# Expert products with 112 stationary columns in place of 128

## The chip, the cores and the metric

The kernel runs on one core of one Trainium2 chip. The metric is the time in device microseconds (us) of one execution; the time before is the median of three runs. TensorE multiplies; VectorE, ScalarE and GpSimd do elementwise work; SyncE issues the transfers from device memory.

## What is computed

The model has a batch of one, 256 tokens of width 1024 and two layers of a first block (half feed-forward layers, attention in the even layer, an RWKV-7 mixer in the odd one), followed by a second block of two layers: a mixer of pooling and convolution, a layer norm, then a dense SwiGLU in layer 0 and a mixture of experts in layer 1, a layer norm and a gated per-layer input. The change is in the mixture of experts:

```python
def moe_swiglu(h, w_router, w1, w3, w2):
    t = h.reshape(B * S, D)                                  # 256 tokens, D = 1024
    logits = (t @ w_router).astype(jnp.float32)
    top_vals, top_idx = lax.top_k(logits, TOP_K)             # 2 of 8 experts for each token
    top_w = jax.nn.softmax(top_vals, axis=-1)
    gates = jnp.sum(jax.nn.one_hot(top_idx, N_EXPERTS) * top_w[..., None], axis=1)
    out = jnp.zeros_like(t)
    for e in range(N_EXPERTS):                               # hidden width D_FF_EXPERT = 3584
        out = out + gates[:, e:e + 1] * swiglu_2(t, w1[e], w3[e], w2[e])
    return out.reshape(B, S, D)
```

All is in fp32. The expert weights alone are 8 x 3 x 1024 x 3584 numbers, 352 MB of the 610 MB that the kernel moves.

## The kernel before, in words

**Rounded fp32 in three products.** Every large product is made of operands in a rounded fp32 type that TensorE streams in one pass. ScalarE writes the rounded high part of a weight block (`split_hi`, line 421), VectorE the rest (`split_lo`, line 429), and `mm3` (line 448) issues three matmuls through `mm` (line 439): high by high, high by low, low by high. Each matmul instruction has a weight load (LDWEIGHTS, PEld in the rows) of the stationary operand, then the moving operand is streamed. In the expert products the moving operand is the weights, 512 columns wide, and the stationary one is the tokens of one expert.

**The stream of weights.** The SyncE queue (line 3561) loads units of 1024 KB into five raw slots, each load waiting until the unit that held its slot has been split. Each unit is split in two halves of 128 x 1024, and four buffers of split halves stand between the splitting engines and TensorE (semaphores `w_hi_ready`, `w_ready`, and `w_read` back).

**Two ways through the experts.** `route_vector` finds the two experts of each token and the largest number of tokens that any expert has, and compares it with `tile_limit`. `either` loads the flag on each compute engine. If it is set, the general way runs (`all_tensor` and its partners): every expert is applied to all 256 tokens. If not, the own way runs (`own_tensor`, `own_scalar`, `own_vector`): the tokens of an expert are gathered into at most 128 slots by products with a 0/1 matrix (`own_gather_tensor`, two experts at a time), and the results are scattered back by products with its transpose, the missing slots being zeros in it.

**The order of the work in the own way.** An expert has 14 blocks of 256 hidden columns, so there are 112 iterations. For each block n, TensorE runs `products(n, 0)` (12 matmuls: 4 depth tiles of 128, three each, into one 512-column bank for both w1 and w3), `turn(n - 1)` (two plain fp32 transposes of the activated block, line 3266), `products(n, 1)` (12 matmuls), and `down(n - 1)` (12 matmuls: 2 halves of the block, 2 halves of the 1024 outputs, three each). Scatters come in four blocks after some experts, a gather in one block of every second expert. ScalarE applies silu (line 3386), rounds the turned block (3356), and copies the gated output y (3373); VectorE multiplies by the w3 half (3436), subtracts for the low part of the turned block (3407) and of y (3414), and adds scattered parts (3424). These read and write all 128 rows of their tiles. The last block has its own `last_down` and `last_scatter`.

The three places where an expert's tokens are the stationary operand are in `products`, `down` and `last_down`. Their column count is 128 whatever number of slots is taken.

Of the kernel before, what the change touches and what calls it, by code (L numbers as in the profile page):

```python
# [13 lines left out]
P = 128  # L14
D = 1024
T = 256
KT = D // P
# [4 lines left out]
CHUNK = 256  # L22
# [17 lines left out]
PAD_POOL = 16  # L40
ALPHA = 4.0 ** 0.25
ARENA = 23296
RAW_SLOTS = 3
MORE_SLOTS = 2
MORE_RAW_AT = 9 * KT * T
# [188 lines left out]
class Kernel:  # L234


    def __init__(self, nc, ctx, dram, out):
# [3 lines left out]
        def sb(name, cols, dtype=F32):  # L241
            return ctx.enter_context(nc.sbuf_tensor(name, [P, cols], dtype))
# [7 lines left out]

        self.raw = sb("raw_weights", RAW_SLOTS * UNIT)
        def sb_rounded(name, cols):
# [20 lines left out]
        self.arena_at = nc.sbuf_base  # L273
        self.arena = sb("arena", ARENA)
        self.x_hi, self.x_lo = self.rounded_arena("own_x_hi", 3, KT * T), self.rounded_arena("own_x_lo", 7, KT * T)
# [11 lines left out]
        mixes = [self.arena[:, at * UNIT:(at + 1) * UNIT] for _, _, at in AFTER_MIXES.values()]  # L287
        self.raw_slots = [self.raw[:, i * UNIT:(i + 1) * UNIT] for i in range(RAW_SLOTS)] + more + mixes
        self.slot_landed = [sem(f"slot_landed{i}") for i in range(RAW_SLOTS + MORE_SLOTS + len(AFTER_MIXES))]
        self.w_hi_ready, self.w_ready, self.w_read = sem("weights_hi_ready"), sem("weights_ready"), sem("weights_taken")  # L290
# [49 lines left out]
    def place_units(self):  # L340

        first = min(n for n, (name, _, _) in enumerate(self.stream) if name.startswith("exp_"))
        self.first_wide = first
        turn = [RAW_SLOTS + i for i in range(MORE_SLOTS)] + [(first - len(AFTER_MIXES) + i) % RAW_SLOTS for i in range(RAW_SLOTS)]
        self.slot, self.landing, self.before = [], [], []
        held = [[] for _ in self.raw_slots]
        placed = 0
        for n, (name, i, _) in enumerate(self.stream):
            if (name, i) in AFTER_MIXES:
                slot = RAW_SLOTS + MORE_SLOTS + list(AFTER_MIXES).index((name, i))  # L350
            else:
                slot = placed % RAW_SLOTS if n < first else turn[(n - first) % len(turn)]
                placed += 1
# [94 lines left out]
def mm3(k, dst, w, at, src, src_at, start, stop, shared, moving_weights=False):  # L448
    for i, (a, b) in enumerate(((0, 0), (0, 1), (1, 0))):
        lhsT, rhs = (src[b][:, src_at], w[a][:, at]) if moving_weights else (w[a][:, at], src[b][:, src_at])  # L450
        ins = mm(k, dst, lhsT, rhs, start and i == 0, stop and i == 2, shared)
    return ins
# [464 lines left out]
EXPERT_UNITS = D_FF_EXPERT // CHUNK  # L917
# [87 lines left out]
class AttentionTiles:  # L1005
    def __init__(self, k):
# [10 lines left out]
        at += 4 * T  # L1017
        self.work = k.arena[:, at:ARENA]
        cols = 2 * N_GROUPS * T + 4
# [442 lines left out]
class RwkvTiles:  # L1462
    def __init__(self, k):
# [14 lines left out]
        self.root, self.inverse = k.arena[:, at:at + 8], k.arena[:, at + 8:at + 16]  # L1478
        self.masks = k.arena[:, ARENA - N_RW_MASK * RW_CHUNK:ARENA]
        self.tmp, self.kk, self.kk2 = (k.xn[:, 2 * i * T:2 * (i + 1) * T] for i in range(3))  # L1480
# [895 lines left out]
def tap_matrix(k, i):  # L2376
    at = ARENA - 4 * TE_TAPS * P
    return k.arena[:, at + i * P:at + (i + 1) * P]
# [450 lines left out]
E = N_EXPERTS  # L2829
# [408 lines left out]
def own_tensor(k):  # L3238
    t = MoeTiles(k)
    mt, sc, ve = k.own_mm, k.own_act, k.own_dve  # L3240
    ident = k.con("ident")
    banks = OwnBanks(k, START_BANKS)
    spare_bank = banks.next

    def products(n, part):

        e, i = divmod(n, EXPERT_UNITS)
        bank = k.bank[4 + n % 2]
        for s in range(2):
            j = k.half[EXPERT_IN, 2 * n + part, s]  # L3250
            k.pe.wait_ge(k.w_ready, j + 1)
            if i == 0 and e % 2 == 0:
                k.pe.wait_ge(*sc.at(("gathered", e // 2, 2 * part + s)))
                k.pe.wait_ge(*ve.at(("gathered", e // 2, 2 * part + s)))
            for k2 in range(2):
                kt = 4 * part + 2 * s + k2
                at = kt * T + e % 2 * P
                ins = mm3(k, bank[:, :], k.weights(j), slice(k2 * 2 * CHUNK, (k2 + 1) * 2 * CHUNK),
                          t.tokens[e // 2 % 2], slice(at, at + P), kt == 0, kt == KT - 1, False, True)
            ins.then_inc(k.w_read, 1)  # L3260

    def turn(n):
        k.pe.wait_ge(*ve.at(("product", n)))
        bank = spare_bank(ve.at(("hidden", n)))
        for i in range(2):
            ins = k.pe.transpose(bank[:, i * P:(i + 1) * P], k.act_buf[:, n % 2 * T + i * P:n % 2 * T + (i + 1) * P], ident)  # L3266
        ins.then_inc(*mt.step(("turned", n)))

    def down(n):
        e, i = divmod(n, EXPERT_UNITS)  # L3270
        y0 = 2 * (e % 2)
        for s in range(2):
            j = k.half[EXPERT_DOWN, n, s]
            k.pe.wait_ge(k.w_ready, j + 1)
            k.pe.wait_ge(*ve.at(("hidden", n)))
            if i == 0 and s == 0 and e >= 2:
                k.pe.wait_ge(*ve.at(("y", e - 2, 1)))
            for c in range(2):
                at = n % 2 * T + s * P
                ins = mm3(k, k.bank[y0 + c][:, :], k.weights(j), slice(c * 512, (c + 1) * 512), k.hidden,  # L3280
                          slice(at, at + P), i == 0 and s == 0, i == EXPERT_UNITS - 1 and s == 1, True, True)
            ins.then_inc(k.w_read, 1)

    def last_down():
        halves = [k.half[EXPERT_DOWN, last, s] for s in range(2)]
        k.pe.wait_ge(k.w_ready, halves[1] + 1)
        k.pe.wait_ge(*ve.at(("hidden", last)))
        for c in range(2):
            for s in range(2):
                at = last % 2 * T + s * P  # L3290
                ins = mm3(k, k.bank[2 * ((E - 1) % 2) + c][:, :], k.weights(halves[s]), slice(c * 512, (c + 1) * 512),
                          k.hidden, slice(at, at + P), False, s == 1, True, True)
            ins.then_inc(*mt.step(f"y{c}"))

    def last_scatter():
        e, before = E - 1, SCATTER_AFTER[E - 1] - 1
        for c in range(2):
            for tt in range(TT):
                u = 2 * c + tt
                k.pe.wait_ge(*ve.at(("z", before, u)))  # L3300
                if c:
                    k.pe.wait_ge(*ve.at(("y", e, tt)))
                moe_z_tensor(k, u, False)
            k.pe.wait_ge(*ve.at(("y", e, c)))
            k.pe.wait_ge(*sc.at(("back", e)))
            for tt in range(TT):
                for low in range(2):
                    ins = mm(k, k.bank[SUM_BANKS[2 * c + tt]][:, :], t.back[e % 4][:, tt * P:(tt + 1) * P],
                             quarter(t.y_own[e % 2][low], c), False, low == 1, True)
                ins.then_inc(k.moe_summed, 1)  # L3310

    def scatter(g, u):
        bank, group = spare_bank(ve.at(("z", g, u))), SCATTERED[g]
        for e in group:
            c, tt = divmod(u, 2)
            if tt == 0:
                k.pe.wait_ge(*ve.at(("y", e, c)))
                k.pe.wait_ge(*sc.at(("back", e)))
            for low in range(2):
                ins = mm(k, bank[:, :], t.back[e % 4][:, tt * P:(tt + 1) * P], quarter(t.y_own[e % 2][low], c),  # L3320
                         e == group[0] and low == 0, e == group[-1] and low == 1, True)
        ins.then_inc(*mt.step(("z", g, u)))

    last = E * EXPERT_UNITS - 1
    for n in range(last + 1):
        e, i = divmod(n, EXPERT_UNITS)
        if n >= 2:
            k.pe.wait_ge(*ve.at(("product", n - 2)))
        products(n, 0)
        if n > 0:  # L3330
            turn(n - 1)
        products(n, 1)
        if n > 0:
            down(n - 1)
        if e - 1 in SCATTER_AFTER and 3 <= i < 7:
            scatter(SCATTER_AFTER[e - 1], i - 3)
        if i == GATHER_AT and e % 2 and e < E - 1:
            own_gather_tensor(k, t, e // 2 + 1, banks)
    turn(last)
    per_layer_input_tensor(k, 1, 0, 1)  # L3340
    last_down()
    last_scatter()
    per_layer_input_tensor(k, 1, 1, 3)
# [217 lines left out]
        k.sp.dma_start(k.raw_slots[k.slot[n]][0:rows, 0:cols], src).then_inc(k.slot_landed[k.slot[n]], 16)  # L3561


def bass_macaron_attention_rwkv_conv_moe_kernel(nc, dram, out, tile_limit=P):
    with ExitStack() as ctx:
        k = Kernel(nc, ctx, dram, out)
        for real in (False, True):
            k.begin(real)
            tensor_program(k)
            scalar_program(k)  # L3570
            vector_program(k, tile_limit)
            gpsimd_program(k)
            sync_program(k)
# [93 lines left out]
```

## Time and profile before

| what | value |
|---|---|
| median of 3 runs | 2622.1 us (2621.82 to 2622.3) |
| span of the profiled execution, first to last instruction | 2622.8 us |
| TensorE busy, share of the span | 2590.1 us, 99% |
| VectorE, ScalarE, GpSimd busy | 2029.8, 1604.4, 237.8 us |
| moved by DMA | 609.58 MB, mean 232 GB/s |

The profiled execution's own time is its span, 0.7 us above the median. The last two fifths of the span, from about 1600 us, are the experts; there the slices of the page show 349 to 375 GB/s, the last one excepted, and TensorE at nine tenths or more in each slice. In rows of the trace, PE is a matmul and PEld the load of its stationary operand; `128*128` is rows by stationary columns, and the shape behind it that of the moving operand. The end of a matmul is modelled and overlaps the next one's start, so the distance between starts tells the pace, not the duration.

### The profile page before, as it was taken

To read this page: it belongs to the slowest core of one execution; us is meant where nothing else is said; L and a number is where in the kernel's file an instruction comes from. 1 tells how busy PE (TensorE), PEld (TensorE's weight loads), DVE (VectorE), ACT (ScalarE), POOL (GpSimd) and SP (SyncE) were. 2 spreads that over 40 slices of the span, in tenths; PEclk is the share of its full clock that TensorE was granted. 3 is DMA by queue.
4 is the path that set the end of the run, shared out by engine and by line. 5 is a ranking of instruction groups with operands and counts; after the bars stand their busy time and mean duration, and the time that the engine had idled before them with its cause. 6 is when DMAs were issued, how large, how long until landed. Compare 5 with 4: busy or idle time off the path is not lost.

```text
span 2622.8 us, 42218 instructions
## 1 busy us (share of the span) xinstructions
PE 2590.1 (99%) x17004; PEld 2230.8 (85%) x17004; DVE 2029.8 (77%) x2919; ACT 1604.4 (61%) x2362; POOL 237.8 (9%) x236
## 2 busy tenths in 40 slices
PE   8999999999999999999999999999999999999999
PEld 7999899999977779999888888888888888888887
DVE  6667676776755547668756787999999999999997
ACT  5557655555542235553555536887788778787875
POOL 1101000000111208002510010000000000000000
PEclk9999999999999999999999999999999999999999
DMA  7554355455321134562455535999999999999994
GB/s 268 188 183 146 111 193 179 175 193 193 126 97 51 66 126 170 180 226 104 173 185 189 188 136 200 375 368 351 361 365 369 349 349 371 372 364 353 373 365 164
DMA packets 85383, 609.58 MB, mean 232 GB/s; under 512 B 9608, under 2 KB 9864, under 8 KB 12224
## 3 DMA queue, kind: packets, MB, share of 16 engines
q1 hardware_dynamic: 82080, 594.58, 61.9%
q10 hardware_dynamic: 2752, 9.09, 1.0%
q8 instruction: 138, 2.26, 0.3%
q0 software_dynamic: 352, 3.15, 0.3%
q14 instruction: 61, 0.50, 0.1%
HBM read 605.73 MB, written 1.05 MB: 231 GB/s over the span
## 4 chain that ended last, share of the span: by engine, by line
PE 94%; DVE 4%; ACT 1%; issue 1%; DMA 0%; ACTq 0%; DVEq 0%
PE bank L439 93%; PE bank L3266 1%; DVE weights_lo L429 0%; ACT weights_hi L421 0%; DMA x_T<-in_x 0%; DVE mean L580 0%; PE bank L2139 0%; DVE rstd L496 0%; DVE weights_hi_scratch L2323 0%; ACT squares L478 0%; DVE weights_hi_scratch L2283 0%; DVE arena L589 0%; DVE x_T L905 0%; DVE arena L2625 0%; DVE source L663 0%
## 5 line engine op out<-in xcount | busy, mean ns | idle before, releaser
L429 DVE TENSOR_TENSOR weights_lo<-raw_weights,weights_hi 128x1024 fp32r<-128x1024 f32 x816 | 1003.0, 1249 | 358.0 <-ACT weights_hi L421 352.5
L421 ACT CAST weights_hi<-raw_weights 128x1024 fp32r<-128x1024 f32 x816 | 847.5, 1050 | 302.7 <-PE bank L439 284.2
L439 PE MATMUL bank<-source,weights_hi 128*128 128x512 f32 (+1 forms) x2464 | 613.7, 365 | 13.7 <-ACT weights_hi L421 10.1
L439 PEld LDWEIGHTS bank<-source,weights_hi 128*128 128x128 f32 x2464 | 412.8, 190 | 60.4 <-ACT weights_hi L421 10.1
L439 PE MATMUL bank<-weights_hi,source 128*128 128x512 f32 (+1 forms) x1280 | 387.3, 386 | 1.5 <-DVE source L663 1.0
L439 PE MATMUL bank<-source,weights_lo 128*128 128x256 f32 x2112 | 380.4, 282 | 0.0
L439 PEld LDWEIGHTS bank<-source,weights_lo 128*128 128x128 f32 x2112 | 338.3, 190 | 37.7 <-DVE weights_lo L429 0.3
L429 DVE TENSOR_TENSOR weights_lo<-arena,weights_hi 128x1024 fp32r<-128x1024 f32 x278 | 335.9, 1224 | 30.7 <-ACT weights_hi L421 27.1
L421 ACT CAST weights_hi<-arena 128x1024 fp32r<-128x1024 f32 x278 | 292.2, 1053 | 50.7 <-PE bank L439 36.1
L439 PEld LDWEIGHTS bank<-weights_hi,source 128*128 128x128 f32 x1280 | 231.5, 188 | 45.4 <-issue 3.1
L439 PE MATMUL bank<-weights_lo,source 128*128 128x512 f32 (+1 forms) x640 | 243.4, 380 | 0.0
L439 PE MATMUL bank<-weights_hi,hidden_hi 128*128 128x512 f32 x536 | 209.2, 390 | 0.0
L439 PE MATMUL bank<-weights_lo,hidden_hi 128*128 128x512 f32 x536 | 208.7, 389 | 0.0
L439 PE MATMUL bank<-hidden_hi,weights_hi 128*128 128x256 f32 x736 | 208.7, 284 | 0.0
L439 PE MATMUL bank<-weights_hi,hidden_lo 128*128 128x512 f32 x536 | 208.7, 389 | 0.0
L439 PE MATMUL bank<-hidden_lo,weights_hi 128*128 128x256 f32 x736 | 208.3, 283 | 0.0
L439 PE MATMUL bank<-hidden_hi,weights_lo 128*128 128x256 f32 x736 | 208.2, 283 | 0.0
L439 PE MATMUL bank<-weights_hi,other_source_hi 128*128 128x512 f32 x448 | 180.4, 403 | 0.0
L439 PE MATMUL bank<-weights_lo,other_source_hi 128*128 128x512 f32 x448 | 175.5, 392 | 0.0
L439 PE MATMUL bank<-weights_hi,other_source_lo 128*128 128x512 f32 x448 | 174.6, 390 | 0.0
L439 PE MATMUL bank<-arena,raw_weights 128*128 128x256 f32 (+2 forms) x592 | 145.6, 397 | 0.0
L439 PEld LDWEIGHTS bank<-hidden_hi,weights_hi 128*128 128x128 f32 x736 | 141.2, 192 | 0.5 <-issue 0.3
(350 smaller groups left out, 3382.4 us busy)
## 6 DMA issues: line engine op xcount, KB each, us to landing
raw_weights<-in_exp_in SPq DMA_DIRECT2D x134, 1024.0 KB, 6.5
arena<-in_exp_in SPq DMA_DIRECT2D x90, 1024.0 KB, 6.7
raw_weights<-in_exp_w SPq DMA_DIRECT2D x67, 1024.0 KB, 6.6
arena<-in_exp_w SPq DMA_DIRECT2D x45, 1024.0 KB, 6.6
raw_weights<-in_ffn_w_down SPq DMA_DIRECT2D x44, 1024.0 KB, 4.9
raw_weights<-in_ffn_w_up SPq DMA_DIRECT2D x43, 1024.0 KB, 4.8
raw_weights<-in_ffn_w_gate SPq DMA_DIRECT2D x42, 1024.0 KB, 4.8
raw_weights<-in_dense_w SPq DMA_DIRECT2D x33, 1024.0 KB, 4.8
```

The lines of the kernel that those rows point to most:

```text
L421: k.act.copy(k.weights(j)[0], raw_half(k, j)).then_inc(k.w_hi_ready, 1)
L429: k.dve.tensor_tensor(lo, raw_half(k, j), hi.bitcast(F32), ALU.subtract).then_inc(k.w_ready, 1)
L439: return k.pe.matmul(dst, lhsT, rhs, start=start, stop=stop, skip_group_check=shared)
L3266: ins = k.pe.transpose(bank[:, i * P:(i + 1) * P], k.act_buf[:, n % 2 * T + i * P:n % 2 * T + (i + 1) * P], ident)
```

## The change

The stationary operand of the expert products takes the first 112 slots in place of 128, and the results are written to the first 112 partitions of their banks. The limit above which the general way is taken is 112 tokens in place of 128. Gathers, transposes, scatters and the work of the other engines keep their shapes; partitions 112 to 127 of the banks keep what was in them, and their slots have zeros in the scattering matrix.

```diff
--- before.py
+++ after.py
@@ -40,6 +40,7 @@
 PAD_POOL = 16
 ALPHA = 4.0 ** 0.25
 ARENA = 23296
+OWN_SLOTS = 112
 RAW_SLOTS = 3
 MORE_SLOTS = 2
 MORE_RAW_AT = 9 * KT * T
@@ -3255,8 +3256,8 @@
             for k2 in range(2):
                 kt = 4 * part + 2 * s + k2
                 at = kt * T + e % 2 * P
-                ins = mm3(k, bank[:, :], k.weights(j), slice(k2 * 2 * CHUNK, (k2 + 1) * 2 * CHUNK),
-                          t.tokens[e // 2 % 2], slice(at, at + P), kt == 0, kt == KT - 1, False, True)
+                ins = mm3(k, bank[0:OWN_SLOTS, :], k.weights(j), slice(k2 * 2 * CHUNK, (k2 + 1) * 2 * CHUNK),
+                          t.tokens[e // 2 % 2], slice(at, at + OWN_SLOTS), kt == 0, kt == KT - 1, False, True)
             ins.then_inc(k.w_read, 1)
 
     def turn(n):
@@ -3277,8 +3278,8 @@
                 k.pe.wait_ge(*ve.at(("y", e - 2, 1)))
             for c in range(2):
                 at = n % 2 * T + s * P
-                ins = mm3(k, k.bank[y0 + c][:, :], k.weights(j), slice(c * 512, (c + 1) * 512), k.hidden,
-                          slice(at, at + P), i == 0 and s == 0, i == EXPERT_UNITS - 1 and s == 1, True, True)
+                ins = mm3(k, k.bank[y0 + c][0:OWN_SLOTS, :], k.weights(j), slice(c * 512, (c + 1) * 512), k.hidden,
+                          slice(at, at + OWN_SLOTS), i == 0 and s == 0, i == EXPERT_UNITS - 1 and s == 1, True, True)
             ins.then_inc(k.w_read, 1)
 
     def last_down():
@@ -3288,8 +3289,8 @@
         for c in range(2):
             for s in range(2):
                 at = last % 2 * T + s * P
-                ins = mm3(k, k.bank[2 * ((E - 1) % 2) + c][:, :], k.weights(halves[s]), slice(c * 512, (c + 1) * 512),
-                          k.hidden, slice(at, at + P), False, s == 1, True, True)
+                ins = mm3(k, k.bank[2 * ((E - 1) % 2) + c][0:OWN_SLOTS, :], k.weights(halves[s]),
+                          slice(c * 512, (c + 1) * 512), k.hidden, slice(at, at + OWN_SLOTS), False, s == 1, True, True)
             ins.then_inc(*mt.step(f"y{c}"))
 
     def last_scatter():
@@ -3561,7 +3562,7 @@
         k.sp.dma_start(k.raw_slots[k.slot[n]][0:rows, 0:cols], src).then_inc(k.slot_landed[k.slot[n]], 16)
 
 
-def bass_macaron_attention_rwkv_conv_moe_kernel(nc, dram, out, tile_limit=P):
+def bass_macaron_attention_rwkv_conv_moe_kernel(nc, dram, out, tile_limit=OWN_SLOTS):
     with ExitStack() as ctx:
         k = Kernel(nc, ctx, dram, out)
         for real in (False, True):
```


## Rows read from the trace of the kernel before

**Rows 1.** The page: span, busy time of each engine, and the chain that ended last.

```profile
span 2622.8 us, 42218 instructions
...
PE 2590.1 (99%) x17004; PEld 2230.8 (85%) x17004; DVE 2029.8 (77%) x2919; ACT 1604.4 (61%) x2362; POOL 237.8 (9%) x236
...
PE 94%; DVE 4%; ACT 1%; issue 1%; DMA 0%; ACTq 0%; DVEq 0%
```

**Rows 2.** Busy us by stretch in plain units; then PEclk, DMA share, GB/s.

```profile
1912.40:2038.90 126.50, 126.50 (x571) 103.92 (x571) 119.27 (x127) 103.99 (x122) 0.00 (x0) 1.00 0.98 367
```

**Rows 3.** The waits, 1700 to 2400 us; last line the DMA queue's: total, times, longest.

```profile
ACT weights_hi L421 <- PE bank L439: 53.2, 142, 1.3
DVE weights_lo L429 <- ACT weights_hi L421: 42.8, 124, 2.0
...
SPq L3561 <- DVE weights_lo L429: 617.6, 240, 7.5
```

**Rows 4.** The chain of waits in order of time: start us, us, what.

```profile
1633.54 0.22 PE bank L3266 x2
1633.75 8.21 PE bank L439 x36
1641.97 0.22 PE bank L3266 x2
```

**Rows 5.** Timeline of TensorE, first product and last: start us, us, what.

```profile
1607.64 0.71 PE L439 MATMUL bank<-weights_hi,source 128*128 128x512 f32 x2
...
2583.70 0.39 PE L439 MATMUL bank<-weights_lo,hidden_hi 128*128 128x512 f32 x1
```

**Rows 6.** Timeline of TensorE in one unit.

```profile
2004.79 0.38 PE L3266 MATMUL bank<-consts,activated 128*128 128x128 f32 x2
...
2005.24 0.40 PE L439 MATMUL bank<-weights_hi,other_source_lo 128*128 128x512 f32 x1
2005.47 0.40 PE L439 MATMUL bank<-weights_lo,other_source_hi 128*128 128x512 f32 x1
...
2007.78 0.39 PE L439 MATMUL bank<-weights_hi,hidden_hi 128*128 128x512 f32 x1
...
2010.50 0.39 PE L439 MATMUL bank<-weights_hi,other_source_hi 128*128 128x512 f32 x1
```

**Rows 7.** Timeline of TensorE, matmuls of 256 columns in the first layer.

```profile
105.17 0.28 PE L439 MATMUL bank<-hidden_lo,weights_hi 128*128 128x256 f32 x1
...
106.97 0.28 PE L439 MATMUL bank<-hidden_lo,weights_hi 128*128 128x256 f32 x1
```

**Rows 8.** Timeline of TensorE, plain fp32 matmuls.

```profile
965.69 5.34 PE L439 MATMUL bank<-arena,raw_weights 128*128 128x256 f32 x24
970.87 1.89 PE L439 MATMUL bank<-arena 128*128 128x256 f32 x8
```

**Rows 9.** Weight loads over the span by form: count, busy us, mean ns, idle.

```profile
L439 PEld LDWEIGHTS bank<-weights_hi,hidden_hi 128*128 128x128 f32 x536 | 100.6, 188 | 21.4 <-issue 0.5 <-DVE weights_lo L429 0.3
...
L439 PEld LDWEIGHTS bank<-arena,raw_weights 128*128 128x128 f32 x544 | 98.3, 192 | 15.7 <-issue 1.8
...
L439 PEld LDWEIGHTS bank<-weights_lo_scratch 64*64 64x64 f32 x496 | 21.4, 135 | 2.9 <-issue 1.6 <-DVE weights_lo_scratch L2280 0.7 <-DVE weights_lo_scratch L2266 0.5
```

**Rows 10.** Timeline of weight loads in the same unit.

```profile
2007.78 0.19 PEld L439 LDWEIGHTS bank<-weights_hi,hidden_lo 128*128 128x128 f32 x1
```

**Rows 11.** Groups of VectorE by form, 1700 to 2400 us: busy, mean ns, idle.

```profile
L429 DVE TENSOR_TENSOR weights_lo<-arena,weights_hi 128x1024 fp32r<-128x1024 f32 x192 | 232.1, 1224 | 19.4 <-ACT weights_hi L421 17.0
...
L3407 DVE TENSOR_TENSOR hidden_lo<-bank,hidden_hi 128x256 fp32r<-128x256 f32 x80 | 33.4, 417 | 0.0
L3436 DVE TENSOR_TENSOR activated<-activated,bank 128x256 f32<-128x256 f32 x80 | 33.1, 414 | 0.0
...
L3414 DVE SCALAR_TENSOR_TENSOR own_y_lo<-bank,arena,own_y_hi 128x512 fp32r<-128x512 f32 x12 | 8.9, 746 | 0.0
```

## Prediction

> **What bounds the kernel now.** I read the page first: of a span of 2622.8 us TensorE is busy 2590.1, and the chain of work that ended last is 94% TensorE, nearly all of it the matmul helper [rows 1]. A busy share alone says little here, since matmul records overlap, so I went on to the stage that the change touches. The busy time by stretch shows, inside the expert loop, TensorE busy all of the time at a granted clock of 1.00 (its 2.4 GHz level), VectorE 94%, ScalarE 82%, and the DMA engines 98% at 367 GB/s: three resources stand close together, and the order has to be settled by waits [rows 2]. Between 1700 and 2400 us TensorE has no line in the list of waits at all. ScalarE waits 53.2 us for it (buffers of split weights that it has to give back), VectorE 42.8 us for ScalarE, and the DMA queue 617.6 us for VectorE to free a raw slot [rows 3]. So everything is paced by TensorE, and DMA has no wait of its own to give away: nobody waits for a landing. The chain repeats 36 matmuls in 8.21 us and two transposes in 0.22 us, from 1633.54 to 1641.97, a **unit of 8.43 us** [rows 4]. There are 8 x 14 = 112 such units, from 1607.64 to the last product at 2583.70 [rows 5]. The few units with a gather or scatter in them are longer by work that the change leaves alone.
>
> **What one matmul costs.** In the quiet half of a unit 12 matmuls start between 2007.78 and 2010.50: 0.2267 us each [rows 6]. 512 columns at 2.4 GHz are 0.2133 us, so 13.3 ns of each is something else. Matmuls of the same rounded type with 256 columns start every 0.120 us (15 from 105.17 to 106.97 [rows 7]); 256 columns are 0.1067, so the rest is again 13.3 ns: a price for each matmul, not for each moving column. Plain fp32 matmuls go through twice and start every 0.216 us (24 from 965.69 to 970.87 [rows 8]), which leaves only 2.5 ns. They load 128 columns too. After the two transposes the matmuls start further apart, 0.23 us or more (2005.24 to 2005.47), and from there to 2007.78 ten take 2.31 us, 0.231 each, before the pace settles at 0.2267 [rows 6]. By the arithmetic a unit is 0.218 for transposes, 36 x 0.2133 = 7.68 for streaming, and **0.535 us of remainder**.
>
> **The change, part by part.** Rounded and plain fp32 operands both stand as f32 in the rows; names tell them apart (arena with raw_weights is plain).
> Part 1, the loads. 4032 products (24 + 12 for each of 112 units) load 112 stationary columns for 128. A load of 128 columns takes 188 ns, one of 64 columns (plain fp32) 135 ns: 0.83 ns a column [rows 9]. I expect 188 - 13 = 175 ns. But a load starts together with a matmul (both at 2007.78) and has 0.227 us until the next [rows 6, 10]: even the 188 ns lie beside the stream with 39 to spare. Taken by itself this is worth nothing.
> Part 2, the 13.3 ns. No row has a rounded matmul with a load of other than 128 columns, so its dependence must be bounded. Below: it is a fixed handover of the array and nothing is saved, 0 us. Above that: it is what the load takes from the moving stream while both read, and goes with the loaded columns. Two things speak for this: the type that streams once leaves 13.3 ns and the one that streams twice, with slack, 2.5; and after a disturbance of the alignment (the transposes) the price is 18 ns for a while (0.231 less 0.2133), which a fixed handover would not show. Then 16/128 of 13.3 is 1.67 ns, x 4032 = **6.7 us**. The ends of this: with the 2.5 ns held fixed and the rest of the remainder scaled, (0.535 - 0.090)/8 x 112 = 6.2; with all of it scaled, 0.535/8 x 112 = 7.5. I take 6.7, the settled half of the unit being the cleanest row.
> Part 3, a quicker kind of load that could be lost. The loads of rounded and plain fp32 take 188 and 192 ns, and the step from 64 to 128 columns is the full 0.83 ns a column, so no faster kind of load is at work now that 112 columns could lose [rows 9]; my sum has no loss here. The Trainium skill ("TensorE: Matmul & The Clock Gate", Weight-path perf modes) says that a fast weight load is on only with exactly 128 stationary columns of a type that isn't FP32; if it were on here, this change would switch it off and loads could grow fourfold. These rows speak against it.
> Part 4, the rest. Matmuls write 112 partitions and stream the same 512 columns: 0. Transposes, gathers, scatters, ScalarE's and VectorE's reads stay at 128 rows: 0. No wait, semaphore or DMA is added or moved. The limit in the flag's comparison is another constant: 0, if the flag stays low (below).
> Part 5, who is late next. A unit shorter by 0.06 us (8.37) needs what the others can give: VectorE needs 6 x 1.224 + 0.417 + 0.414 = 8.175 us in a plain unit [rows 11], cover 0.26 now and 0.20 after; DMA at 98% allows about 2%, 0.17 us. Both still cover it. The two units in an expert with the 0.75 us of the lower half of y [rows 11] already run VectorE over a unit's length, and the four weight buffers carry it.
> Sum against the profiled 2622.8: -6.7, 2616.1. The median of the three runs shown is 2622.1, 0.7 less; on it **2615.4 us**. What a measurement can tell from no change is 0.2%, 5.2 us, so my term is just outside.
>
> **Rivals.**
> A, the forecast: the 13.3 ns go with the columns, 2614.6 to 2615.9.
> B, a fixed price: loads are 175 ns in the trace, but starts stay 0.2267 apart: 2622, give or take 1. For it: the settled value is the same to a tenth of a ns for 256 and 512 columns, as a handover would be. Against it: the unsettled 18 ns, the 2.5 of plain fp32.
> C, more than in proportion: 13.3 ns is also just what 16 columns take at 0.83 ns each, so if the stream waited for the last columns of a load, all of it could go, 4032 x 13.3 = 54 us. Against it stand the 39 ns of cover. It would not be given whole: DMA at 98% caps the stage of 976 us near 2%, 19 us, then ScalarE waits for landings: 2603.
> D, slower: the array must run empty when the column count changes, 128 to 112 and back around each pair of transposes. Place: before the transposes and before the first product after them. Price: a matmul's record lasts 0.39 us and the next starts after 0.227, so 0.16 us of it is overlap that an emptying lays bare [rows 6]; twice a unit, 224 x 0.16 = 36 us, 2658. It decides from 0.024 us an occurrence on. Against it: going from plain transposes back to rounded products costs now no such gap, from 2004.79 to 2005.24 there are 0.45 us for work of 0.43 [rows 6]. The Trainium skill ("TensorEngine Tiling (Array Packing)", Key Properties) says that a change of tiling mode drains TensorE; 112 columns are over 64 and so no other mode by its list, and no row here has 112.
> E, the change takes the other branch: with an expert above 112 tokens the general way runs. A unit is then 96 products of 0.120 and 24 of 0.227, 17.0 us for 8.43 [rows 6, 7], x 112 = 955 us more, 3577. The trace tells only that no expert has over 128. Worked out from the reference with its own first inputs the counts are 84, 108, 48, 52, 68, 36, 70, 46: 108 fits with four to spare. Other seeds of the same inputs give 128, 131 and 121, so this is a risk of the data.
>
> **How the numbers follow.** A 0.43, B 0.40, C 0.06, D 0.08, E 0.03. The likeliest is A, its own range 2614.6 to 2615.9. A and B together are 0.83, so the range needs both with their spread, 2614 to 2623.5; I take the low end down to 2611, since the ten unsettled matmuls of a unit may gain more than in proportion, and stop before C. Faster by over 0.2%: A but for a hundredth, and C, 0.48. Within: B and that hundredth, 0.41. Slower: D and E, 0.11.
>
> **What would show it.** In the profile after: 4032 loads at about 175 ns with 112 columns; in the quiet half of a unit starts 0.225 apart (A) or 0.2267 (B); a unit of 8.37 or 8.43; TensorE still without waits. C would show starts near 0.22 with ScalarE waiting for DMA. D would show 0.16 us gaps beside the transposes at line 3266, E the groups of the general way. I am wrong in the mechanism if loads don't shorten, or if the unit shortens while the quiet half's spacing does not.

## The result and the profile after

The changed kernel takes **2641.8 us** (median of 5 runs, 2639.4 to 2643.1) against 2622.1 (5 runs, 2621.8 to 2622.4): ratio **1.007**, 95% interval 1.006 to 1.0081. It is slower by 19.7 us where 6.7 less were forecast. The own way still runs. Profile against profile, one execution of each kernel, the spans differ by 17.6 us. The page of the kernel after, answering to [rows 1]:

```profile
span 2640.4 us, 42218 instructions
...
PE 2607.3 (99%) x17004; PEld 2177.6 (82%) x17004; DVE 2036.6 (77%) x2919; ACT 1603.1 (61%) x2362; POOL 238.1 (9%) x236
```

The same number of instructions; loads are busy 53 us less, and matmuls 17 us more. The weight loads by form, answering to [rows 9], and the busy time of the stretch of [rows 2]:

```profile
L440 PEld LDWEIGHTS bank<-weights_hi,hidden_hi 128*112 128x112 f32 x448 | 78.0, 174 | 25.8 <-issue 0.3 <-DVE weights_lo L430 0.3
```

```profile
1912.40:2038.90 126.50, 126.50 (x560) 94.90 (x559) 117.28 (x123) 100.78 (x119) 0.00 (x0) 1.00 0.97 361
```

A load takes 174 ns for 188, as it should. TensorE is again busy all of the time at its 2.4 GHz level, with 560 matmuls in the stretch for 571. Nobody else became late: VectorE, ScalarE and DMA all do less in the same time. The waits from 1700 to 2400 us, answering to [rows 3], have no line with TensorE waiting either:

```profile
ACT weights_hi L422 <- PE bank L440: 57.2, 142, 1.3
DVE weights_lo L430 <- ACT weights_hi L422: 46.8, 128, 2.0
```

So the matmuls themselves are slower. The chain, answering to [rows 4], and TensorE's timeline in the quiet half of a unit, answering to [rows 6]:

```profile
1694.09 0.22 PE bank L3267 x2
1694.30 8.39 PE bank L440 x36
1702.70 0.22 PE bank L3267 x2
```

```profile
2005.91 0.39 PE L440 MATMUL bank<-weights_hi,other_source_lo 128*112 128x512 f32 x1
2006.15 0.40 PE L440 MATMUL bank<-weights_lo,other_source_hi 128*112 128x512 f32 x1
2006.38 0.39 PE L440 MATMUL bank<-weights_hi,hidden_hi 128*112 128x512 f32 x1
2006.61 0.39 PE L440 MATMUL bank<-weights_hi,hidden_lo 128*112 128x512 f32 x1
...
2008.01 0.39 PE L440 MATMUL bank<-weights_hi,hidden_lo 128*112 128x512 f32 x1
```

The transposes still take 0.22 us, but the 36 products 8.39 us for 8.21: a unit is **8.61 us for 8.43**. From 2005.91 to 2008.01 nine matmuls start 0.2333 us apart, not 0.2267. The time above streaming has gone from 13.3 to 20.0 ns a matmul. In full resolution the starts follow a pattern of three distances, near 237, 231 and 232 ns, that runs through a whole unit and begins again after each pair of transposes. In the mean over the 36 products of a unit the distance has grown by 5.0 ns, not by 6.7, since 12 of the 36 stood at some 231 ns before. Of the 111 stretches from one pair of transposes to the next, 80 are 8.61 us, 14.3 us of the loss; all 111 together are 17.0 us longer.

One more thing stands in the same trace. After each of the three later gathers some units are quicker, with the very same instructions on the same tiles. The chain at such a place:

```profile
1811.38 8.26 PE bank L440 x36
1819.64 0.22 PE bank L3267 x2
1819.86 8.24 PE bank L440 x36
...
1836.80 8.40 PE bank L440 x36
```

Units of 8.46 and 8.48 us turn into one of 8.61 with nothing in the program different. The count of columns alone can't be the cause; the same matmuls run in one steady pattern or in another.

### The profile page after: what moved, and what is told of

The parts are those of the page before. It is cut to its first block, busy times and chain, and to the rows that moved or that the text cites. A ratio compares the mean times of both kernels' runs of the same rounds, so it can differ in the third digit from the quotient of the medians.

```text
span 2640.4 us, 42218 instructions
## 1 busy us (share of the span) xinstructions
PE 2607.3 (99%) x17004; PEld 2177.6 (82%) x17004; DVE 2036.6 (77%) x2919; ACT 1603.1 (61%) x2362; POOL 238.1 (9%) x236
## 4 chain that ended last, share of the span: by engine, by line
PE 94%; DVE 4%; ACT 1%; issue 1%; DMA 0%; POOL 0%; ACTq 0%; DVEq 0%
PE bank L440 92%; PE bank L3267 1%; DVE weights_lo L430 0%; ACT weights_hi L422 0%; DMA x_T<-in_x 0%; ACT squares L479 0%; DVE mean L581 0%; POOL squares L976 0%; PE bank L2140 0%; DVE rstd L497 0%; DVE weights_hi_scratch L2324 0%; DVE weights_hi_scratch L2284 0%; DVE arena L590 0%; DVE x_T L906 0%; DVE arena L2626 0%
## 5 line engine op out<-in xcount | busy, mean ns | idle before, releaser
L440 PE MATMUL bank<-weights_hi,source 128*112 128x512 f32 (+2 forms) x1280 | 389.2, 387 | 1.5 <-DVE source L664 1.0
L440 PEld LDWEIGHTS bank<-weights_hi,source 128*112 128x112 f32 (+1 forms) x1280 | 219.9, 179 | 59.2 <-issue 3.1
L440 PE MATMUL bank<-weights_lo,source 128*112 128x512 f32 (+2 forms) x640 | 245.4, 383 | 0.0
L440 PE MATMUL bank<-weights_lo,hidden_hi 128*112 128x512 f32 (+1 forms) x536 | 212.3, 396 | 0.0
L440 PE MATMUL bank<-weights_hi,hidden_hi 128*112 128x512 f32 (+1 forms) x536 | 211.3, 394 | 0.0
L440 PE MATMUL bank<-weights_hi,hidden_lo 128*112 128x512 f32 (+1 forms) x536 | 210.3, 392 | 0.0
L440 PE MATMUL bank<-weights_hi,other_source_hi 128*112 128x512 f32 x448 | 181.0, 404 | 0.0
L440 PE MATMUL bank<-weights_lo,other_source_hi 128*112 128x512 f32 x448 | 177.5, 396 | 0.0
L440 PE MATMUL bank<-weights_hi,other_source_lo 128*112 128x512 f32 x448 | 176.0, 393 | 0.0
```

Of the source, the lines that this page charges most:

```text
L440: return k.pe.matmul(dst, lhsT, rhs, start=start, stop=stop, skip_group_check=shared)
```

## The experiments

"Unit" below is the time from one pair of transposes to the next in a plain block, the median over an expert's plain units in the trace. The sweeps give each of the eight experts its own column count and first column; slots outside an expert's columns are left out of its products, and only the distances between starts are read. Each sweep has one profiled execution.

**How many columns.** The edit, here for s1 (s2 has 128, 100, 96, 88, 80, 72, 64, 48):

```diff
-OWN_SLOTS = 112
+COLS = (128, 124, 120, 116, 112, 108, 104, 96)
...
-                ins = mm3(k, bank[0:OWN_SLOTS, :], k.weights(j), slice(k2 * 2 * CHUNK, (k2 + 1) * 2 * CHUNK),
-                          t.tokens[e // 2 % 2], slice(at, at + OWN_SLOTS), kt == 0, kt == KT - 1, False, True)
+                ins = mm3(k, bank[0:COLS[e], :], k.weights(j), slice(k2 * 2 * CHUNK, (k2 + 1) * 2 * CHUNK),
+                          t.tokens[e // 2 % 2], slice(at, at + COLS[e]), kt == 0, kt == KT - 1, False, True)
```

> One kernel, eight column counts: experts 0 to 7 take 128, 124, 120, 116, 112, 108, 104 and 96 stationary columns in their products (limit for the general way back at 128; slots above an expert's count are left out of its products, and the trace is read, not the time). What is read is the mean distance between matmul starts in each expert's plain units. The trace of the changed kernel has 233.3 ns at 112 and 226.7 at 128. Theory 1, quadrants: a column count that isn't a multiple of 32 is dear, so 128 and 96 give 226.7 and all between 233. Theory 2, length: the price of a load on the moving stream changes steadily with its length, so the distance grows from 128 (226.7) over 120 (230) to 112 (233.3) and on to 104 (237) and 96 (240). Theory 3, lock: load and stream fall into a repeating pattern that depends on the count in no steady way; then the values jump, 112 is 233.3, and some counts repeat every three matmuls. Theory 4, drain at the change of shape: all distances inside a unit 226.7 and the loss beside the transposes; the trace after already speaks against it.

> As s1, with 128, 100, 96, 88, 80, 72, 64 and 48 columns for experts 0 to 7 (slots above that are left out). Theory 1, quadrants: 128, 96 and 64 at 226.7, the others near 233. Theory 2, length: 96 at 240, growing below. Theory 3, lock: jumps, no order. If what remains is the load's own reading taken from the stream, 64 and 48 must lie clearly below 226.7 (half the columns, at most 220).

Measured units, us: 128: **8.433**; 124: 8.444; 120: 8.608; 116: 8.607; 112: **8.613**; 108: 8.506; 104: 8.463; 100: 8.607; 96: 8.500; 88: 8.40 and 8.60; 80: 8.620; 72: 8.530; 64: 8.502; 48: 8.653. The 88 columns have no one value: their units alternate. The chain in s2:

```profile
1997.17 8.39 PE bank L443 x36
2005.56 0.22 PE bank L3270 x2
2005.78 8.18 PE bank L443 x36
```

The loads shorten evenly, 188 ns at 128 to 122 at 48. Theory 1 falls (96 and 64 are not 8.433), so does theory 2 (104 is better than 112, 100 worse than both), and with it the forecast: at 48 columns the distance is larger than at 128, so what a load reads isn't what the stream loses. Jumps without order are theory 3. The chain around a unit of 120 columns in s1:

```profile
1936.21 0.22 PE bank L3270 x2
1936.42 8.40 PE bank L443 x36
1944.82 0.22 PE bank L3270 x2
```

**Where the columns lie.** s3 and s6 add a first column other than 0:

```diff
-                at = kt * T + e % 2 * P
+                at = kt * T + e % 2 * P + FROM[e]
```

> Same number of columns, other place: experts 0 to 7 take (columns from offset) 128 from 0, 112 from 0, 112 from 16, 112 from 8, 112 from 4, 120 from 8, 96 from 0, 96 from 32, so that some loads end where the load of 128 ends; products then hold other slots than they should, with the same amount of work. Theory 5, place: the load is read from its last column or its price hangs on where it ends, so 112 from 16 and 120 from 8 give 226.7 and 112 from 0 gives 233.3, with 8 and 4 in between or elsewhere. Theories 1 to 3: the offset doesn't matter, all four of 112 give 233.3 and both of 96 the same.

> Finer steps and other starts, experts 0 to 7 (columns from offset): 126, 122, 118, 114, 110 from 0, then 120 from 4, 124 from 4, 116 from 12 (other slots than they should have in the last three). Lock theory: values between 226.7 and 236 in no order, neighbours of 2 columns differing by several ns, and for the same 120 columns a third value beside 233.3 (from 0) and 226.7 (from 8). A rule of the end (a load that ends on a multiple of 512 bytes is cheap) would give 226.7 for 124 from 4 and 116 from 12; 112 from 16 with 231.7 speaks against it already. A rule of the start would give 120 from 4 the 233.3 of 112 from 4.

Units, by the byte within the 512 of a slot block at which the load ends:

| ends at | columns from first column: unit, us |
|---|---|
| 512 | 128 from 0: 8.433; 124 from 4: 8.407; 120 from 8: 8.407; 116 from 12: 8.407; but 112 from 16: 8.555; 96 from 32: 8.555 |
| 496 | 124 from 0: 8.444; 120 from 4: 8.444 |
| 480 | 120 from 0: 8.608; 112 from 8: 8.608 |
| 464 | 116 from 0: 8.607; 112 from 4: 8.607 |

(126, 122, 118, 114 and 110 from 0: 8.620, 8.543, 8.566, 8.513, 8.603.) The same 120 columns give 8.608, 8.444 or 8.407. The chain for expert 5 of s3, 120 columns from 8, against that of s1 above, 8.19 for 8.40:

```profile
2313.55 0.22 PE bank L3270 x2
2313.77 8.19 PE bank L443 x36
2321.96 0.22 PE bank L3270 x2
```

Loads of different length that end at the same byte agree to a nanosecond a matmul or better in the mean, down to 116 columns at 512; the place of the start doesn't do that. The exception is kept: below 116 columns the end at 512 is no longer cheap, and 112 from 16 and 96 from 32 share another value. The forecast in s3 that 112 from 16 is cheap was a miss.

**Which products, which order.** In s4 only the products (`COLS`) or only the down products (`DOWN_COLS`) of an expert are narrowed; in s7 `mm3` takes its three products in another order:

```diff
-    for i, (a, b) in enumerate(((0, 0), (0, 1), (1, 0))):
+    for i, (a, b) in enumerate(order):
```

> Which products carry it: experts 0 to 7 take (gate and up products / down products) 128/128, 112/128, 128/112, 112/112, 112/112, 96/128, 128/96, 96/96 columns (slots above are left out). If the price belongs to each matmul with 112 columns, an expert with 112 only in the 24 gate and up products loses 24/36 of the full loss of 0.18 us a unit, 0.12, and one with 112 only in the 12 down products 0.06. If it is a lock that runs on over the whole unit, the two don't add up: the 128-column part is slower than 226.7 too while its partner is 112, or the 112-column part is not slow at all.

> Same loads and streams, other order of the three products of a group (in the kernel: high stationary x high moving, low x high, high x low). Experts 0 to 7: 128 columns in the orders hh hl lh, lh hh hl, lh hl hh (stationary named first); 112 columns in the same three; 120 and 108 columns in the first. If the price is the number of columns or of partitions written, order changes nothing: 226.7 at 128 and 233.3 at 112, in all orders. If it is a lock between the addresses or types that follow each other, values move: I expect one of the orders of 112 at another steady value (229 to 236) and 128 to lose its 226.7 in one of them.

s4: 112/128 8.526, 128/112 8.460, 112/112 8.613, against 8.433. The losses 0.093 and 0.027 don't add up to 0.180, nor are they 0.12 and 0.06: a matmul's price hangs on those around it. The other mixes say the same: 96/128 8.467, 128/96 8.493, 96/96 8.500. In 128/96 the down products alone run at about 230 ns. s7: nothing moves, 8.433 in all orders of 128, 8.613 in all of 112, 8.611 for 120 and 8.507 for 108. My expectation there was wrong; which rounded part follows which plays no role.

**The limit alone.**

```diff
-def bass_macaron_attention_rwkv_conv_moe_kernel(nc, dram, out, tile_limit=P):
+def bass_macaron_attention_rwkv_conv_moe_kernel(nc, dram, out, tile_limit=112):
```

> The other half of the change by itself: 128 columns, the flag's limit at 112. If the whole loss is the column count, this is the kernel before: 2622, ratio 1.000 within 0.001, a unit of 8.433 us. If the limit costs anything (another constant in one comparison), part of the 20 us shows here.

2622.7 us against 2622.7, ratio 1.000 (0.9991 to 1.001). The column count carries all.

**The address, without touching the columns.** A pad moves tiles in on-chip memory; s8 is a sweep with the pad, s9 has 128 columns throughout:

```diff
+        sb("pad_source", 8)
         source, scratch = sb_rounded("source", 2 * KT * T)
```

> A pad of 8 numbers (32 bytes a partition) ahead of the tokens' tile, so that this and every later tile lies 32 bytes further, while the split weights stay. Experts 0 to 7: 128, 124, 120, 116, 112 from 0, 112 from 16, 108, 96 columns. If the address of the stationary operand (against the weights or absolutely) decides, 120 now starts where 120 from 8 did and gives 226.7 and a unit of 8.407 in place of 233.3 and 8.608, and 128 may lose its 226.7. If only the place inside the 128 slots or the count decides, all values are those of s1: 226.7, 228, 233.3, 233.3, 233.3, 231.7, 230, 230.

> The kernel before, 128 columns everywhere, with only the 32-byte pad ahead of the tokens' tile. Theory of the address: the load of 128 columns then ends 32 bytes past a multiple of 512, as expert 0 of s8 (8.620 us a unit for 8.433), so this kernel loses 0.187 x 100 plain units and a like share of the others, about 20 us, 2642, as much as the change itself, with no column fewer. Other layers keep or move a little. Theory of the count: 2622, no difference.

s8: 128: 8.620; 124: 8.620; 120: 8.433; 116: 8.453; 112: 8.620; 112 from 16: 8.539; 108: 8.613; 96: 8.487. The quick place has moved with the pad, from 128 columns to 120, which now end at 512. It isn't quite the 8.407 that was expected from s3 for the same 120 columns: there only the reads of the products moved, here all later tiles did. s9 is the kernel before with the pad and nothing else; the chain in its experts:

```profile
1966.42 0.22 PE bank L3271 x2
1966.64 8.40 PE bank L444 x36
1975.04 0.22 PE bank L3271 x2
```

This kernel has not a column fewer than the one before and nearly the unit of the changed one, 8.62 us for 8.61. From the first transposes of the experts to the last it takes 982.0 us, where the kernel before takes 961.9 and the changed one 978.9: the loss of 20 us is there as forecast. Its time is 2634.9, ratio 1.0051 (1.0035 to 1.0066), not 2642, since the experts begin at 1604.1 us, where they begin between 1613.1 and 1617.2 in the profiles of all kernels with the tiles in their old places. So the other layers gained 9 us or more by the same pad, and their columns are the same, too; only addresses differ. Which operands make the other layers quicker was not looked into.

**One operand's address or the distance of the two.** s10 has the pad ahead of the split weights, so both operands move; s11 places the split weights behind the other tiles with 32 bytes before them, so that among the operands of the products only the moving one changes its place within 512 bytes. It also comes to lie some 139 KB further in the memory by the sizes in the kernel, the tiles ahead of it 32 KB less far, and the small tiles behind it (constants, the activated block) move by the 32 bytes, too; no run has that without the 32 bytes.

> The pad of 32 bytes ahead of the split weights, so that the moving and the stationary operands both lie 32 bytes further and keep their distance. Experts 0 to 7: 128, 124, 120, 116, 112, 108, 104, 96 columns. If the distance between the two operands decides, the values of s1 come back: 8.433 at 128, 8.608 at 120, 8.613 at 112. If the stationary operand's own address decides, those of s8: 8.620 at 128, 8.433 at 120, 8.620 at 112.

> Only the split weights (the moving operand) lie 32 bytes further against a multiple of 512; the stationary tiles keep theirs. Experts as in s10. If the stationary address alone decides, the values of s1 (8.433, 8.444, 8.608, 8.607, 8.613, 8.506, 8.463, 8.500). If the distance decides, others: 128 loses its 8.433.

| columns | 128 | 124 | 120 | 116 | 112 | 108 | 104 | 96 |
|---|---|---|---|---|---|---|---|---|
| s1, nothing moved | 8.433 | 8.444 | 8.608 | 8.607 | 8.613 | 8.506 | 8.463 | 8.500 |
| s10, both by 32 bytes | 8.433 | 8.444 | 8.611 | 8.607 | 8.613 | 8.506 | 8.463 | 8.500 |
| s8, stationary by 32 | 8.620 | 8.620 | 8.433 | 8.453 | 8.620 | 8.613 | - | 8.487 |
| s11, moving by 32 | 8.620 | 8.607 | 8.613 | 8.506 | 8.470 | 8.387 | 8.520 | 8.607 |

The same 116 columns in s1, s10, s8 and s11, one unit's products of the chain each:

```profile
1988.05 8.39 PE bank L443 x36
```

```profile
1988.60 8.39 PE bank L444 x36
```

```profile
1999.80 8.23 PE bank L444 x36
```

```profile
1991.00 8.29 PE bank L444 x36
```

Row two repeats row one in eight of eight places, and moving either operand against the other breaks it: the **distance between the two operands** counts, not where the pair of them lies. s11 is mostly row one moved by 8 columns (32 bytes) to the left: 124 has 116's value, 120 has 112's, 116 has 108's, 112 nearly 104's. That also speaks against the 139 KB as the cause. It fails at 108 (8.387, where 100 columns had 8.607), so the end of the load isn't all of the rule. These two values are near the two between which the 88 columns of s2 alternate, and the 96 columns of s11 have a unit of 8.389 before they settle at 8.607, so a place can have two steady patterns; whether the miss at 108 is a case of that is not shown.

**The change itself, made quicker by an address.** s13 is the changed kernel with the weights placed as in s11, and so with the same reservation.

> The changed kernel as it is, 112 columns and limit 112, only with the split weights 32 bytes further against a multiple of 512. The theory of the distance gives the unit of s11's expert 4, 8.470 us for the 8.613 of the changed kernel: about 100 plain units x 0.143 = 14 us, and with the other layers 4 us faster or so (s11 began its experts at 1611.9), about 2624, ratio to the kernel before near 1.001. If 112 columns are slow by themselves, it stays at 2638 or more.

2624.5 us, ratio to the kernel before 1.0011 (1.0002 to 1.0021), as forecast, for 1.007 of the changed kernel without this. Its chain, 8.25 for 8.39:

```profile
1968.19 0.22 PE bank L3271 x2
1968.41 8.24 PE bank L444 x36
1976.66 0.22 PE bank L3271 x2
1976.88 8.25 PE bank L444 x36
```

**Versions meant to beat both.** s12 keeps the slots in columns 8 to 127 (the place of each slot is raised by 8 before the 0/1 matrix is made, the transposes write from column 8, the scatter takes 120 rows), so that 120 columns end at 512. s14 is simpler, `sb("pad_source", 8)` and 120 columns from 0.

```diff
-OWN_SLOTS = 112
+OWN_SLOTS = 120
+SKIP = P - OWN_SLOTS
...
-                at = kt * T + e % 2 * P
+                at = kt * T + e % 2 * P + SKIP
```

> A version by the theory: 120 slots, limit 120, kept in columns 8 to 127 of the 128, so that every expert load has 120 columns and ends on a multiple of 512 bytes. By s3 (expert 5) a unit is then 8.407 us for 8.433 before: 0.026 x 112 = 2.9 us less than before and 0.206 x 112 = 23 less than after: 2619 against 2622, ratio 0.999. If the address were no cause, 120 columns would give the 8.608 of s1 and 2641.

> A version that should beat both kernels: the 32-byte pad ahead of the tokens' tile, which in s9 brought the experts' start forward from 1616 to 1604 us, and 120 columns from 0 (limit 120), which with this pad end on the multiple of 512 again and gave a unit of 8.433 in s8. Then the experts take the 962 us of the kernel before and the rest the 1604 + 46 us of s9: 2612 to 2614, ratio 0.996 to 0.997. If the gain of the other layers in s9 was chance, 2622.

s12: 2619.5 us, ratio 0.999 (0.9981 to 0.9999), on the forecast. But no settled unit has the forecast 8.407: they are 8.387 in some stretches and 8.427 in others, and only their mean is right, which is in part luck. The chain within the fourth expert, ahead of its gather and behind it:

```profile
2009.37 8.18 PE bank L441 x36
```

```profile
2064.86 8.22 PE bank L441 x36
```

s14: **2617.7 us, ratio 0.9981 (0.9972 to 0.999)**, the lowest median of the study (the intervals of s12 and s14 overlap), and 0.991 of the changed kernel's. Both gains over the kernel before are small, and s12's is barely clear of none. s14 missed its forecast by 4 us: the profiled execution has the span of 2613.3 and the parts as forecast (experts from 1605.3, 962.5 us long), but its runs scatter from 2614.2 to 2619.7. Its experts, and its matmuls of 256 columns in the first layer, answering to [rows 7]:

```profile
1969.13 8.23 PE bank L444 x36
1977.36 0.22 PE bank L3271 x2
1977.58 8.21 PE bank L444 x36
```

```profile
105.72 0.28 PE L444 MATMUL bank<-hidden_lo,weights_hi 128*128 128x256 f32 x1
...
107.12 0.28 PE L444 MATMUL bank<-hidden_lo,weights_hi 128*128 128x256 f32 x1
```

Twelve starts in 1.40 us are 116.7 ns each for the 120.0 of the kernel before: at 256 columns the settled 13.3 ns are not a floor, here they are 10.0. At 512 columns the settled distance of s14 is still 226.7.

**How far the distance counts.** The pad at 64 and 96 bytes:

> Tiles of tokens 64 bytes further, experts 0 to 7: 128, 124, 120, 116, 112, 108, 104, 96 columns from 0. If the distance counts modulo 64 bytes, all values of s1 come back. If it counts in a longer period, 112 now ends at 512 and should give the 8.555 of 112 from 16 (s3), and 104 that of 120 from 0 or near it (8.608); 128 ends at 576, unknown.

> Tiles 96 bytes further, same counts. With a period of 64 bytes the values of s8 come back (8.620 at 128, 8.620 at 124, 8.433 at 120, 8.453 at 116, 8.620 at 112, 8.613 at 108, 8.487 at 96). With a longer one 104 ends at 512, others unknown. The start of the experts shows what this place does to the other layers: 1604 as in s9, 1616 as before, or another.

s15, 128 to 96 columns: 8.622, 8.613, 8.608, 8.607, 8.556, 8.440, 8.523, 8.605, and the experts begin at 1601.0 us. s16: 8.653, 8.573, 8.618, 8.618, 8.540, 8.400, 8.553, 8.612, and 1621.0. (Medians; in both runs the 112 and the 96 columns have units in two patterns, up to 0.18 us apart.) Neither s1 nor s8 comes back, so the period is longer than 64 bytes. In s15 the 112 columns end at 512 and have the 8.556 that s3 had for the same distance. Against the 1613 to 1617 of the old places, the other layers are some 11 us better at 32 bytes, 14 better at 64 and 6 worse at 96, the last two by one execution each.

## Why the prediction was wrong, point by point

**What bounds the kernel: right.** The whole difference is in TensorE's matmul distances; no wait arose, and the other engines and DMA stayed covered.

**Part 1, the loads: right.** 174 ns, forecast 175, and no gain came of it.

**Part 2, the 13.3 ns: the step that failed.** I bounded the unknown price from both sides as 0 (fixed) and -1.67 ns a matmul (in proportion to the columns) and left out that it could rise. It rose, by 6.7 ns in the settled half (13.3 to 20.0) and by 5.0 ns a matmul over a plain unit: a loss of 17.0 us in the experts in place of a gain of 6.7. Both ends rested on the picture of a price that belongs to the load. s1 and s2 show that it doesn't fall with the columns at all, and s3, s8, s10 and s11 that it goes with the distance between the two operands' addresses, since shorter loads from the same first column end 64 bytes earlier. The rows for it stood in the prediction: the same matmuls took 226.7 ns in one half of a unit and 231 in the other [rows 6]. I read that as the load taking from the stream, and as a gain still to be had. Read plainly it says that the price is a state that other arrangements can push up to 18 ns and more, and that the kernel before was in a good one for two thirds of a unit. With that the rows give an upper end: 231 for 226.7 in the 24 quiet matmuls of 112 units, some 12 us slower, on the other side of zero and still short of the 17 measured. The agreement of 13.3 ns at 256 and 512 columns, which made the price look like one for each matmul, was chance of the placement: s9 and s14 have 10.0 at 256 columns, with 20 and 13.3 at 512 in the experts.

**Part 3, the quick load: right** that none was at work to be lost; the loads shortened evenly with their columns, 0.83 ns each down to 48, and 128 is on the same line as the rest. No group of loads has a mean above 217 ns in any trace, so the fourfold growth that the prediction names is shown nowhere.

**Parts 4 and 5: right.** The limit costs nothing (s5), and nobody became late.

**The rivals.** A (0.43) and B (0.40) are both wrong: neither in proportion nor fixed. C wrong in sign. D (0.08) had the sign and not the mechanism: transposes and the first product after them take 0.45 us as before (from 2011.98 to 2012.43), and the loss is in the middle of the products. It was the only slower rival beside E, and the price of the settled state changing was no rival at all. E didn't occur. The chance of 0.11 for slower was too small, since it held no case in which a quantity that I couldn't explain got worse.

**The range** of 2611 to 2623.5 missed by 18 us for the same reason: its upper end was the fixed price.

## What to carry to other kernels

A remainder that you can't explain must be bounded on both sides of its present value, and if the trace shows the same instruction at two paces, both are ends. Before narrowing a stationary operand, read the distance between matmul starts, not busy time: 5.0 ns more a matmul came to 14 us in the plain units alone, where the whole change was to give 6.7. When rounded fp32 matmuls run at 227 to 236 ns for 512 columns, move one operand's tile by 32 or 64 bytes and look again; it costs one line, and here it moved the kernel by some 14 us one way and 6 the other outside the experts and by 20 us inside, so only a run tells which way it goes.

## What the runs showed of the hardware

- In the experts rounded fp32 matmuls of 512 columns, each with its load, start 226.7 ns (the kernel before, settled) to 235.5 ns (48 columns in s2, settled) apart in the mean at the full clock, in patterns that repeat (every three matmuls in the changed kernel). Which one depends on the distance in memory between stationary and moving operand, and, at some distances, on what came before (8.46 and 8.61 us for the same unit in the changed kernel, 8.40 and 8.60 in turn at 88 columns).
- Even the best distances here, 226.7 and 116.7 ns for 512 and 256 columns, are 13.3 and 10.0 ns above streaming. The Trainium skill ("TensorE: Matmul & The Clock Gate", Back-to-back issue gap) gives 2.5 ns above streaming at full clock for the isolated gap, and about 131 ns a matmul of 512 columns for a sustained stream of loads and matmuls. The plain fp32 matmuls agree with the 2.5 ns [rows 8]; the rounded ones agree with neither figure in any run here, and the measurement decides.
- Both operands moved together by 32 bytes change nothing (8 of 8 units within 0.003 us).
- Fewer stationary columns make the load shorter, 0.83 ns a column from 128 down to 48, and the matmul no quicker: 48 columns have the longest unit of s1 and s2.
- By what means the distance of the two operands acts is not shown: they were only moved about. The exact rule (the end of the load fits most points, not 108 columns in s11 or 112 from 16 in s3) stays open, as does its period beyond 64 bytes.
